# Softmax probabilities of two attention layers multiplied by their inverse sums on POOL instead of the vector engine

## What is computed

```python
logits = jnp.where(mask, jnp.einsum('bnqkgd,bnjkd->bnkgqj', qb, kk), -jnp.inf)
m = jnp.maximum(jnp.max(logits, axis=-1, keepdims=True), sink)
e = jnp.exp(logits - m)
probs = e / (jnp.sum(e, axis=-1, keepdims=True) + jnp.exp(sink - m))
out = jnp.einsum('bnkgqj,bnjkd->bnqkgd', probs, vv)
```

## Time and profile before

| | |
|---|---|
| time, median of 3 runs | 2324.14 us (2321.87 to 2325.43) |
| the profiled execution | 2324.22 us, span 2322.4 us |
| granted TensorE clock, mean | 0.982 |
| busy: PE, DVE, ACT, POOL | 95%, 74%, 59%, 2% |
| attention of layer 0, pairs in flight | about 52 to 84 us |
| attention of layer 1 | about 427 to 461 us |
| DMA | 573.37 MB, 247 GB/s in the mean |

### The profile page before, as it was taken

One profiled execution on the slowest core, in us unless ns is written; L12 is line 12 of the kernel. 1 busy time (PEld: TensorE's weight loads), 2 busy tenths in 40 slices (PEclk: granted clock), 3 DMA queues, 4 the chain that ended last, 5 costly groups with the idle time before them and its releaser, 6 DMA issues. The chain is left out here.

```text
span 2322.4 us, 32524 instructions
## 1 busy us (share of the span) xinstructions
PE 2208.4 (95%) x12412; PEld 1891.4 (81%) x12412; DVE 1714.9 (74%) x1892; ACT 1372.5 (59%) x1425; POOL 54.7 (2%) x72
## 2 busy tenths in 40 slices
PE   7899999889999999999999999898899999889998
PEld 5699987668888888888888877688779988878997
DVE  5655457668888888888888889766657767666766
ACT  5533334647777777777777777473454446355544
POOL 2000000020000000000000020000000000000000
PEclk9999999999999999999999999899999999999999
DMA  9555554249999999999999999631335543233551
GB/s 388 195 200 182 183 191 170 100 164 394 369 386 367 383 374 382 372 381 377 377 376 380 369 387 376 232 123 74 108 126 192 182 163 130 73 113 116 183 197 38
DMA packets 81800, 573.37 MB, mean 247 GB/s; under 512 B 9552, under 2 KB 9664, under 8 KB 15984
## 3 DMA queue, kind: packets, MB, share of 16 engines
q1 hardware_dynamic: 76320, 545.82, 61.9%
q0 software_dynamic: 5376, 26.12, 3.0%
HBM read 564.03 MB, written 17.83 MB: 251 GB/s over the span
## 5 line engine op out<-in xcount | busy, mean ns | idle before, releaser
L525 DVE TENSOR_TENSOR w_lo<-raw,w_hi 128x2048 fp32r<-128x2048 f32 x508 | 1163.3, 2300 | 357.4 <-ACT w_hi L520 355.7
L520 ACT CAST w_hi<-raw 128x2048 fp32r<-128x2048 f32 x508 | 969.2, 1911 | 492.9 <-PE bank L770 487.2
L770 PE MATMUL bank<-w_hi,xT_hi 128*128 128x512 f32 x1184 | 468.4, 396 | 8.5 <-DVE w_lo L525 6.6
L770 PE MATMUL bank<-w_hi,xT_lo 128*128 128x512 f32 x1184 | 461.5, 390 | 0.0
L770 PE MATMUL bank<-w_lo,xT_hi 128*128 128x512 f32 x1184 | 461.2, 390 | 0.0
L770 PE MATMUL bank<-xT_hi,w_hi 128*128 128x256 f32 x1344 | 381.3, 284 | 7.7 <-DVE xT_lo L1815 6.5
L770 PE MATMUL bank<-xT_lo,w_hi 128*128 128x256 f32 x1344 | 380.6, 283 | 0.0
L770 PE MATMUL bank<-xT_hi,w_lo 128*128 128x256 f32 x1344 | 380.6, 283 | 0.0
L770 PE MATMUL bank<-w_hi,aT_hi 128*128 128x512 f32 x864 | 345.9, 400 | 15.3 <-DVE aT_lo L2027 9.5
L770 PE MATMUL bank<-w_hi,aT_lo 128*128 128x512 f32 x864 | 338.9, 392 | 0.0
L770 PE MATMUL bank<-w_lo,aT_hi 128*128 128x512 f32 x864 | 338.8, 392 | 0.0
(11 more groups left out here) (321 smaller groups left out, 1672.7 us busy)
## 6 DMA issues: line engine op xcount, KB each, us to landing
raw<-in_wu_eg SPq DMA_DIRECT2D x112, 1024.0 KB, 7.2
raw<-in_wu_eu SPq DMA_DIRECT2D x112, 1024.0 KB, 7.1
raw<-in_wu_ed SPq DMA_DIRECT2D x112, 1024.0 KB, 7.1
raw<-in_wu_up SPq DMA_DIRECT2D x44, 1024.0 KB, 4.8
raw<-in_wu_ffn_gu SPq DMA_DIRECT2D x28, 1024.0 KB, 4.8
raw<-in_wu_in SPq DMA_DIRECT2D x28, 1024.0 KB, 4.8
raw<-in_wu_down SPq DMA_DIRECT2D x22, 1024.0 KB, 4.8
raw<-in_wu_ffn_d SPq DMA_DIRECT2D x14, 1024.0 KB, 4.8
```

The source lines that it names most:

```text
L520: nc.scalar.copy(w_hi[:, place(i), :], src).then_inc(*E.hi.mark("unit", i))
L525: nc.vector.tensor_tensor(w_lo[:, place(i), :], raw[:, i % RAW, :], w_hi[:, place(i), :].bitcast(F32), ALU.subtract) \
L770: mm = nc.tensor.matmul(o, l[i], r[j], start=(first and n == 0), stop=(last and n == 2), skip_group_check=not lone)
```

## The change

In layers 0 and 1 the vector engine now ends its part of `normalise` with the reciprocal and marks a new event, `inverted`. POOL waits for it and does both multiplications, in place in `pr`, and marks `probs`. In POOL's order the eight pairs of a layer stand ahead of the wait for that layer's last scores, and so ahead of the mask and vector loads. Layers 2 and 3 keep their multiplications on the vector engine.

```diff
+        inverted = ev.new("sums_inverted")
...
+            def normalise(L, p):
+                i = p % 2
+                gp.wait_ge(*inverted.at(L, p))
+                for q, (a, c) in enumerate(((0, P), (P, 3 * P))):
+                    pr = att["pr"][:, i, :, a:c]
+                    ins = nc.gpsimd.tensor_tensor(pr, pr, rden[:, i, :, q:q + 1].to_broadcast([P, 2, c - a]), ALU.mult)
+                ins.then_inc(*probs.mark(L, p))
             for L in range(2):
+                for p in range(8):
+                    normalise(L, p)
                 gp.wait_ge(*M.free[1].at("sc", L, 15))
                 load_mask(1 if L == 0 else 3)
...
                 if L == 1:
                     chain(V_.tensor_tensor(rsum[:, i, :, :], rsum[:, i, :, :], esink[:, i, :, :], ALU.add))
+                if L < 2:
+                    V_.reciprocal(rden[:, i, :, :], rsum[:, i, :, :]).then_inc(*inverted.mark(L, p))
+                    return
                 chain(V_.reciprocal(rden[:, i, :, :], rsum[:, i, :, :]))
```

## The result

| | before | after |
|---|---|---|
| median | 2324.44 us (20 runs, 2320.70 to 2327.14) | 2330.18 us (20 runs, 2326.07 to 2334.09) |
| the profiled execution, span | 2324.22, 2322.4 us | 2331.65, 2329.8 us |
| granted TensorE clock, mean | 0.982 | 0.980 |

The ratio is 1.0025, 95% interval 1.0019 to 1.0031: 5.7 us slower. The forecast was 2330.8, with a range of 2327 to 2339. The sum is right, but by luck in part: the delay D was taken too long, TensorE's clock was put at nothing, and the two nearly cancel.

The account below looks back on a forecast made before the run. The prediction took the loop through all engines in the attention of layers 0 and 1, plus layer 1's vector queue, as the bound. 3.55 us and 3.00 us summed to 6.55 on 2324.22, giving 2330.8 us, range 2327 to 2339.

Parts of the forecast that it names:

- D: Time by which a pair's probabilities come later after its reciprocal than before the change; forecast 0.95 us, ends 0.66 and 1.92.
- What bounds: Attention of layers 0 and 1: a loop through all engines, 5.73 us a pass in layer 0; layer 1's vector queue also full.
- Hand-over, 0.27: Vector engine to POOL: first multiplication starts 0.48 us after the reciprocal's start instead of 0.21, so 0.27 later.
- Multiplications, 1.71: A pair's two multiplications on POOL take 1.71 us against 1.03 on the vector engine, reading earlier long additions as taking turns.
- rival 2: POOL really needs the face value, 2.68 us a pair in both attentions: D 1.92, 2338.5 us; chance 0.15.
- POOL to TensorE: Hand-over from POOL's multiplication to TensorE's transposes, taken as 0.05 us, the same as from the vector engine.
- Counting: How often D is passed up to pair 6's transposes: 4D - 0.25 (3.55 us) in layer 0, 4D - 0.80 (3.00) in layer 1.
- 8D - 1.05: Sum of the shifts in the attentions of layers 0 and 1: 6.55 us with D at 0.95.
- Clock 1.00 in the second half of each stretch: Expected sign in both attentions: TensorE's grant stays at 1.00, since pauses of about 1 us kept it in 446 to 454.
- rival 3: TensorE's clock falls in the longer pauses of both attentions: 2335 to 2341 us; chance 0.12.
- POOL's queue: Mask and vector loads behind eight pairs of multiplications come a few us later, which costs nothing; configuration and tiny sums cost nothing.
- Carried to the end whole: After the attentions the weight buffers are full, so nothing runs ahead and the whole shift of 6.55 us reaches the end.

Follow-up runs that it names:

- the doubled work: The changed kernel with POOL multiplying each pair first by one, then by its inverse sum: 2346.23 us, 1.0095 against the kernel before.
- layer 0 alone: The changed kernel with only layer 0's multiplications on POOL, layer 1's kept on the vector engine: 2325.91 us, 1.0007 against the kernel before.
- the filled pause: The changed kernel with three useless products ahead of the transposes of pair 6 in layer 1 only: 2332.27 us, 1.0027 against the kernel before.
- the last filling: The changed kernel with three useless products behind both layers' queries and two ahead of pair 6 in layer 1: 2328.91 us, 1.0019 against the kernel before.
- the first filling alone: The kernel before with three useless products behind the turned queries of both layers, no second batch: 2321.77 us, 0.9988 against the kernel before.

## Why the prediction was right

- *What bounds.* Right. The change made the loop through all engines longer, at a pass of 6.36 = 5.73 + D. That the vector engine's work fell by 14 us was worth nothing but layer 1's queue. The signs in absolute time fit less well than the sum: the transposes of pair 6 came 3.63 later in layer 0 (81.37), of which 0.50 stood there before the first reciprocal, and 5.38 later in layer 1 (459.91), not 6.5.
- *Hand-over, 0.27.* **Wrong: 0.04.** I took the 0.30 of the mask load, though it is a DMA issue. The start was 0.07 after the reciprocal's end, and the other end of the range, 0.02, was nearly right.
- *Multiplications, 1.71.* The mechanism was right, the size 0.10 high: 1.61 (2.26 x 0.75 is 1.70, by the way; the sum took 1.71). The estimate by the figure of the Trainium skill (GPSIMD Engine Reference, 3.1) was 1.69. The face value, 2.68 (rival 2), is out: the long additions of the earlier trace rows were turns, as the split between both engines shows.
- *POOL to TensorE.* Right, 0.06 for 0.05. So D is 0.63 and not 0.95, just below the lower end of 0.66.
- *Counting.* Right for the kernels as they run, with the low grant at the entry of each attention: 8D - 1.05, held up by the doubled work in layer 0 (9.04 for 9.07) and by layer 1 (1.74 for 1.72). With the clock held high it is 2.9 for 4.0, since the relief of the vector engine, "worth nothing" beyond the 0.80 in the prediction, then pays at the entry of layer 1.
- *"Clock 1.00 in the second half of each stretch", pauses of about 1 us.* **Wrong in both layers.** The pause ahead of pair 6 in layer 1, where TensorE has no more scores to do, had been 1.57 and became 1.99. Behind it the grant fell, which cost 1.54. In layer 0 the low grant lasted to about 67.7 instead of 63.6; 0.86 beyond the loops stands there. Part of rival 3 came true together with the forecast, which treated them as exclusive.
- *POOL's queue.* Right. The mask load went from 76.65 to 84.86 and from 452.96 to 462.78, and the next vector load still waited 29.08 us and more for the vector engine. The configuration, a 77 ns instruction, issued at 23.9 and left no mark. "The tiny two-input sums of layer 1 fall into POOL's pauses" holds for all but one: the first took 0.43 instead of 0.16 and ended at 439.60, with POOL's multiplications (439.58).
- *Carried to the end whole.* Right here: the stretch between the layers is 282.30 on both sides, and the splits are 6.89 later behind layer 1's attention and 7.52 at the end. It is no rule: the 3.2 of layer 0 alone were gone at the end of its trace, and the 0.9 of the filled pause by 520 us.

In the sum, the eight D were 2.56 too high (8 x 0.32), and the clock added 2.4 (0.86 + 1.54) that the forecast had at nothing: 6.55 - 2.56 + 2.40 = 6.39, the local sum measured (it closes by construction, for the 2.40 is what the count left over). The forecast's 2330.8 beside 2330.18 owes its closeness to this, and that is luck. **The steps that failed** are the hand-over, mis-sized at 0.27 for 0.04 (1.84 of the 2.56), and the clock, put at nothing and worth 2.4. With its own counting and the true D, but no word of the clock, it would have said 2328.2 (2324.22 + 3.99), 0.17% slower and so "within 0.2%", which is where the prediction had put everything under D = 0.66.

How much is the clock's depends on what one compares with. Held high on both sides, the loops cost 2.02 + 0.89 = 2.9, and of the 6.39 some 3.5 are then the clock's: 1.11 in layer 0 (2.01 - 0.90), 0.85 ahead of pair 6 of layer 1 (1.74 - 0.89), 1.54 behind it.

## What to carry to other kernels

In a loop that runs through several engines, an instruction costs its latency once in each pass, and the utilization of its engine says nothing: count how often the delay is passed, then look for the queue waits that it gives back. A loop made longer also makes TensorE's pauses longer, so check the granted clock behind the longest of them, which here was where the engine had run out of other work. Then look past the place of the change: a shift of a few us moved the clock's low stretches in code that nobody had touched, and these took or gave as much as the experiments were looking for. Compare traces at fixed points, not only whole times. For a hand-over between engines take a row of the same kind of instruction; a DMA issue is not one.

## What the runs showed of the hardware

- A compute instruction on POOL started 0.06 to 0.08 us after the vector instruction that released it ended, where a DMA issue took 0.30. Relayed through a one-element memset on POOL, an event arrived 0.16 later in all.
- POOL's multiplication by a broadcast factor took 0.61 us for 2 x 128 elements in each partition and 1.04 for 2 x 256. Beside a two-input instruction of the vector engine the former took 1.12.
- TensorE's grant stayed at 1.00 through repeated pauses of 1.1 to 1.5 us with work between (the loop in layer 0, also with doubled work) and through one of 1.57. Behind single pauses of 1.81 (clock kept high at the start), 1.99, 2.11 and 2.32 (doubled work) the grant fell to 0.50 for some us. But the length of a pause does not decide it alone: ahead of the turned queries of layer 1 the kernel before waits 1.99 too, and with the useless products behind them the grant was 1.00 from 424 to 432 us and on. These are readings under this program's load, not a rule.
- Three useless products behind the queries (2.7 us on an idle TensorE) kept the clock at 1.00 through the start of both attentions and saved 1.36 us there. The kernel before was 0.7 to 4.9 us faster with them.
- The low stretches behind the attention moved from kernel to kernel in unchanged code: 0.57 in 116 to 120 us with the last filling, 1.00 there in the kernel before with the first filling alone; 0.76 in 345 to 352 in the kernel before, 1.00 with the filling.
